# Values as the stationary operand in a branched attention, with the output scale brought in by two transfers

## The reference

```python
s = einsum('bqghd,bgqmd->bghqm', qb, k_sel) * scale
p = _masked_softmax(s - slopes * dist, dist >= 0)       # e / sum(e)
o_slc = einsum('bghqm,bgqmd->bqghd', p, v_sel)
...
o_win = einsum('bghqk,bkgd->bqghd', p_win, vw)
o = gb[..., 0:1] * o_cmp + gb[..., 1:2] * o_slc + gb[..., 2:3] * o_win
```

## Time and profile before

| | |
|---|---|
| median of 3 runs | 2609.11 us (2608.38 to 2610.36) |
| the profiled execution | 2607.89 us |
| its span | 2606.1 us |
| PE busy, 12947 products | 2545.3 us (98%) |
| DVE / ACT / POOL busy | 1198.0 / 833.9 / 1160.2 us |
| 16 DMA engines, mean | 86 GB/s |

### The profile page before, as it was taken

The page is one execution under the profiler, slowest core; times in us unless marked ns, Lnnn a source line. Parts: engine busy times, 40 slices in busy tenths (PEclk is TensorE's granted clock), DMA queues, the critical chain, the costliest instruction groups (busy, mean ns, idle before and its releaser), DMA issues.

```text
span 2606.1 us, 37755 instructions
## 1 busy us (share of the span) xinstructions
PE 2545.3 (98%) x12947; PEld 2158.3 (83%) x12947; DVE 1198.0 (46%) x2275; ACT 833.9 (32%) x1473; POOL 1160.2 (45%) x586
## 2 busy tenths in 40 slices
PE   7989999999999999999999999999999999999998
PEld 6788888887888888899888788888899888888887
DVE  6556666664432221177775422211477765322211
ACT  4456554664221110144444211100244443211101
POOL 4335430000277788700000777788300002877886
PEclk9989999999999999999999999999999999999999
DMA  7321113333233333322223233333222222333332
GB/s 161 107 41 34 33 42 81 89 89 89 87 97 97 97 95 98 102 66 77 70 83 92 81 97 97 97 97 97 90 78 73 65 87 81 95 96 96 98 95 76
DMA packets 422189, 222.88 MB, mean 86 GB/s; under 512 B 59504, under 2 KB 420268, under 8 KB 422060
## 3 DMA queue, kind: packets, MB, share of 16 engines
q1 hardware_dynamic: 419100, 218.03, 29.5%
q10 hardware_dynamic: 2960, 3.22, 0.4%
HBM read 212.86 MB, written 2.10 MB: 82 GB/s over the span
## 4 chain that ended last, share of the span: by engine, by line
PE 88%; DVE 7%; ACT 3%; issue 2%; DMA 0%; DVEq 0%; ACTq 0%; POOL 0%
PE psA L1063 48%; PE psB L1086 13%; PE psA L1086 10%; PE psA L1319 5%; PE psB L1319 4%; PE psO L967 3%; PE psB L948 2%; PE psB L924 1%; DVE b L2009 1%; DVE b L1669 1%; DVE b L2157 1%; ACT b L2460 1%; DVE b L2049 0%; PE psO L1359 0%; DVE b L2030 0%
## 5 line engine op out<-in xcount | busy, mean ns | idle before, releaser
L1063 PE MATMUL psA<-b,b 128*128 128x512 f32 x5616 | 1286.8, 391 | 3.8 <-DVE b L1458 1.8
L1063 PEld LDWEIGHTS psA<-b,b 128*128 128x128 f32 x5616 | 1054.1, 188 | 234.4 <-issue 8.9
L743 POOL TENSOR_TENSOR b<-b,b 128x1024 fp32r<-128x1024 f32 x239 | 453.5, 1897 | 1201.2 <-PE psA L1063 1041.1
L745 POOL TENSOR_TENSOR b<-b,b 128x1024 fp32r<-128x1024 f32 x239 | 594.1, 2486 | 18.7
L1086 PE MATMUL psB<-b,b 128*128 128x512 f32 (+4 forms) x1626 | 367.6, 384 | 7.7 <-DVE b L1893 4.5
L1086 PEld LDWEIGHTS psB<-b,b 128*128 128x128 f32 (+2 forms) x1626 | 299.6, 196 | 67.9 <-DVE b L1893 4.9
L1086 PE MATMUL psA<-b,b 128*128 128x512 f32 x1356 | 326.2, 396 | 0.0
L1458 DVE SCALAR_TENSOR_TENSOR b<-psA,b 128x512 f32<-128x512 f32 x152 | 104.7, 691 | 461.3 <-PE psA L1063 457.5
L1086 PEld LDWEIGHTS psA<-b,b 128*128 128x128 f32 x1356 | 253.3, 189 | 54.8 <-issue 1.0
L1469 DVE TENSOR_TENSOR b<-b,psA 128x512 f32 x48 | 33.0, 688 | 338.0 <-PE psA L1063 338.0
L2343 ACT ACTIVATE b<-b,b (+1 forms) x56 | 40.5, 724 | 441.1 <-DVE b L1469 434.6
(11 more groups left out here) (271 smaller groups left out, 2177.2 us busy)
## 6 DMA issues: line engine op xcount, KB each, us to landing
b<-in_w_in SPq DMA_DIRECT2D x296, 256.0 KB, 3.1
b<-in_w_ffn_in SPq DMA_DIRECT2D x176, 256.0 KB, 3.1
b<-in_w_ffn_out SPq DMA_DIRECT2D x64, 256.0 KB, 2.9
b<-in_w_out SPq DMA_DIRECT2D x48, 256.0 KB, 3.0
b<-in_w_gate SPq DMA_DIRECT2D x44, 256.0 KB, 3.1
b<-in_w_up SPq DMA_DIRECT2D x44, 256.0 KB, 3.2
b<-in_w_down SPq DMA_DIRECT2D x32, 256.0 KB, 3.0
b<-in_w_ffn_out SPq DMA_DIRECT2D x32, 192.0 KB, 2.5
```

Source lines behind the costliest of these rows:

```text
L743: nc.gpsimd.tensor_tensor(w[:, 0], wraw[:, s], ones[:, 0:1].broadcast_to([P, KT * P]), ALU.mult).then_inc(w_hi.sem, 1)
L745: nc.gpsimd.tensor_tensor(w[:, 1], wraw[:, s], hi_f(w[:, 0]), ALU.subtract).then_inc(w_lo.sem, 1)
L1063: i = mm(dst, w[:, wh, kt * P:(kt + 1) * P], rhs(xh, kt), start=first and kt == 0 and n == 0, stop=last and kt == kts - 1 and n == 2)
```

## The change

`values` keeps `vtok` (key tile by [high | low] columns) stationary and moves `PT`: for each key tile one product over all its queries, 512, 384, 256 and 128 columns, for both halves of `PT`. `psO` then has [high 64 | low 64] on the partitions and the 512 queries in the columns. The scale is therefore needed along the columns, equal on all partitions: `unit_scale` on SP waits for `gate`, writes the 128 x 4 numbers as a row of 512 into HBM, waits for that, and loads the row onto all 128 partitions (256 KB). `scaled` waits for that load. `gate(U + 1)` is placed where `gate(U)` was, `gate(0)` ahead of the loop. POOL adds only the two branches. `pair_output` adds high and low halves by two products with a constant "fold" matrix, whose moving operand is the added output, 512 columns in full precision. SP's order of query copies and weight loads is written anew around the `unit_scale` calls.

```diff
-                  ("slope", HEADS), ("edge", 32), ("lam", 4),
+                  ("slope", HEADS), ("edge", 32), ("lam", 4), ("fold", 3 * HD),
...
+    at = CONST["fold"].start
+    c[:, at + HD:at + 2 * HD] = (p % HD == np.arange(HD)[None])
...
-        om = pl(TT, 2, HD)
+        om = pl(T)
...
+        ow_row = [nc.dram_tensor(f"unit_scale{b}", (T,), F32).ap() for b in range(2)]
...
+        def scale_of(U):
+
+            if U >= 28:
+                return (n_r0, n_r2)[U % 2][:, :]
+            return hi_f(attnT[:, U % 2, 4 if U in (0, 2) else 6, :])
...
+            def unit_scale(U):
+
+                b, o = U % 2, 32 * (U % 2) + 16
+                sp.wait_ge(ug_dve.sem, ug_dve.at(U))
+                sp.dma_start(ow_row[b].rearrange("(q p) -> p q", p=P), st[:, o:o + TT], allow_slow_non_contiguous=True).then_inc(row_out[b], 16)
+                sp.wait_ge(row_out[b], 16 * (U // 2 + 1))
+                sp.dma_start(scale_of(U), ow_row[b].partition_broadcast(P)).then_inc(scale_in[b], 16)
...
-            for n in range(1, 4):
-                query_twice(n)
-                query_load(n + 4)
...
+            unit_scale(0)
+            for n in range(8):
+                unit_scale(4 * n + 1)
+                if n < 7:
+                    query_twice(n + 1, 0)
+                unit_scale(4 * n + 2)
+                if n < 7:
+                    query_twice(n + 1, 1)
+                if n < 3:
+                    query_load(n + 5)
+                else:
+                    lru_weights(n - 3)
+                unit_scale(4 * n + 3)
+                if n < 7:
+                    unit_scale(4 * n + 4)
+            for c in range(5, 4 * KT):
+                lru_weights(c)
...
-                nc.gpsimd.tensor_tensor(ow[0][:, :], ow[0][:, :], ow[1][:, :], ALU.add).then_inc(oa_pool.sem, 1)
-                pool.wait_ge(oa_pool.sem, oa_pool.at(j, "units"))
                 if hd == 0 and n:
                     pool.wait_ge(ot_pe.sem, ot_pe.at(n - 1))
-                parts = ow[0][:, :].rearrange("p (q h d) -> p q h d", h=2, d=HD)
-                nc.gpsimd.tensor_tensor(om[:, :, hd, :], parts[:, :, 0, :], parts[:, :, 1, :], ALU.add).then_inc(oa_pool.sem, 1)
+                nc.gpsimd.tensor_tensor((om, ow[1])[hd][:, :], ow[0][:, :], ow[1][:, :], ALU.add).then_inc(oa_pool.sem, 1)
...
-                    for qt in range(TT):
-                        for kt in range(qt + 1):
-                            at = PT_AT[kt] + (qt - kt) * P
-                            i = mm(psO[:, qt * P:(qt + 1) * P], PT[:, h, at:at + P],
-                                   vtok[:, br, kt, n // 4, hd, :, :].rearrange("p h d -> p (h d)"),
-                                   start=h == 0 and qt == 0, stop=h == 1 and kt == qt, skip_group_check=True)
+                    for kt in range(TT):
+                        at, w = PT_AT[kt], (TT - kt) * P
+                        i = mm(psO[:, T - w:T], vtok[:, br, kt, n // 4, hd, :, :].rearrange("p h d -> p (h d)"),
+                               PT[:, h, at:at + w], start=h == 0 and kt == 0, stop=h == 1 and kt == TT - 1, skip_group_check=True)
...
-                for qt in range(TT):
-                    i = mm(psO[:, qt * P:(qt + 1) * P], om[:, qt, :, :].rearrange("p h d -> p (h d)"), ident,
-                           start=False, stop=qt == TT - 1, skip_group_check=True)
+                for hd in range(2):
+                    at = CONST["fold"].start + (1 - hd) * HD
+                    i = mm(psO[:, :], con[:, at:at + P], (om, ow[1])[hd][:, :], start=False, stop=hd == 1, skip_group_check=True)
...
-                o = 32 * (U % 2)
                 dve.wait_ge(uv_pe.sem, uv_pe.at(U))
-                dve.wait_ge(ug_dve.sem, ug_dve.at(U))
-                if U >= 2:
-                    dve.wait_ge(oa_pool.sem, oa_pool.at(U // 2 - 1, "units" if U % 2 else "parts"))
-                v.tensor_tensor(ow[U % 2][:, :].rearrange("p (q c) -> p q c", c=P), psO[:, :].rearrange("p (q c) -> p q c", c=P),
-                                st[:, o + 16:o + 20].unsqueeze(2).broadcast_to([P, TT, P]), ALU.mult).then_inc(uo_dve.sem, 1)
+                dve.wait_ge(scale_in[U % 2], 16 * (U // 2 + 1))
+                if U % 4 == 1 and U > 4:
+                    dve.wait_ge(ot_pe.sem, ot_pe.at(U // 4 - 1))
+                elif U >= 2:
+                    dve.wait_ge(oa_pool.sem, oa_pool.at(U // 2 - 1))
+                v.tensor_tensor(ow[U % 2][:, :], psO[:, :], scale_of(U), ALU.mult).then_inc(uo_dve.sem, 1)
...
-                gate(U)
+                if U + 1 < 32:
+                    gate(U + 1)
...
+            gate(0)
             for n in range(8):
```

More of the change, by code:

```diff
@@ L447, in build @@
         uo_dve = steps("unit_scaled", ["all"])
-        oa_pool = steps("head_added", ["units", "parts"])
+        oa_pool = steps("head_added", ["units"])
+        row_out = [sem(f"unit_scale_row_stored{b}") for b in range(2)]
+        scale_in = [sem(f"unit_scale_loaded{b}") for b in range(2)]
         cs_pe = steps("compressed_scores", ["all"])
@@ L629, in _, with query_twice @@
                     load(c, c % RAW, [(b, b + 2, w1[:, 4 * s + b:4 * s + b + 2, :]) for b in (0, 2)], wide_rows)
-            def query_twice(n):
-                for hd in range(2):
-                    here, there = (slice(b * HD, (b + 1) * HD) for b in (hd, 1 - hd))
-                    sp.wait_ge(ql_pool.sem, ql_pool.at(n, f"lo{hd}"))
-                    q = query_pair(n, hd)
-                    sp.dma_start(hi_f(q[there, :, :]), hi_f(q[here, :, :])).then_inc(q_twice[hd], 16)
-            query_twice(0)
+            def query_twice(n, hd):
+                here, there = (slice(b * HD, (b + 1) * HD) for b in (hd, 1 - hd))
+                sp.wait_ge(ql_pool.sem, ql_pool.at(n, f"lo{hd}"))
+                q = query_pair(n, hd)
+                sp.dma_start(hi_f(q[there, :, :]), hi_f(q[here, :, :])).then_inc(q_twice[hd], 16)
+            def unit_scale(U):
[4 more added lines that the diff above has]
+                sp.dma_start(scale_of(U), ow_row[b].partition_broadcast(P)).then_inc(scale_in[b], 16)
+            query_twice(0, 0)
+            query_twice(0, 1)
             for n in range(2, 5):
                 query_load(n)
-            for n in range(1, 4):
-                query_twice(n)
-                query_load(n + 4)
             o3 = 2608
@@ L650, in lru_load, with lru_weights @@
                 load(C_LRU + c, c % RAW, parts, dst)
-            for m in range(KT):
-                for x in range(3):
-                    if m == 0:
-                        query_twice(x + 4)
-                    lru_load(4 * m + x, col_tile(w_in, KT, m * P + o3 + x * D))
-                if m == 0:
-                    query_twice(7)
-                lru_load(4 * m + 3, [(b, 0, woa[b, :, :, m * P:(m + 1) * P]) for b in range(2)],
-                         lambda slot, b: slot[b * HD:(b + 1) * HD, :, :])
+            def lru_weights(c):
+                m, x = divmod(c, 4)
+                if x < 3:
+                    lru_load(c, col_tile(w_in, KT, m * P + o3 + x * D))
+                else:
+                    lru_load(c, [(b, 0, woa[b, :, :, m * P:(m + 1) * P]) for b in range(2)],
+                             lambda slot, b: slot[b * HD:(b + 1) * HD, :, :])
+            unit_scale(0)
[8 more added lines that the diff above has]
+                    query_load(n + 5)
+                else:
+                    lru_weights(n - 3)
[4 more added lines that the diff above has]
+                lru_weights(c)
             def gate_load(m):
```

## The result

The changed kernel takes **2783.4 us** (median of 4 runs, 2780.3 to 2787.1) against 2609.1: ratio 1.067, with a 95% interval of [1.065, 1.068], 174 us slower.

The account below looks back on a forecast made before the run. TensorE was taken to set the attention's pace, busy 29.7 of a group's 30.1 us. Shorter work -26, clock -6 and transfers +2 gave -30 us from 2609.1: 2579 us, forecast 2570 to 2588, range 2563 to 2600.

Parts of the forecast that it names:

- The two transfers: Each unit's gate to HBM and back over all partitions: 4.2 to 9.2 us, taken as 6; 2 us charged in all.
- Rival 4: Transfers set the attention's pace, two units taking the chain plus 6.0 us; at 11 us chain 22 us slower, 2631; chance 0.08.
- The cover: Time from the gate's place to the scaling that needs it: 9.8 and 8.6 us, about 7 left to hide the transfers.
- over 7 us together: Stated failure condition: the forecast falls if a unit's two transfers together take more than 7 us.
- Values: A unit's twenty value products become eight: block 1.25 us, 0.94 less; second and third units get all of it.
- Fold: Per group, four passes of 512 columns replace eight of 128: 0.43 us each, 0.83 us more in the second unit.
- Gate: Reciprocal and gate a unit earlier: ScalarE's copy less late, at most 1.3 us in first units, about 0.4 in fourth.
- VectorE's share: VectorE's busy part of an attention group was to rise from 71% to 79% and meet some of the gain.
- rival 1: The chain stays: copy and subtraction end no earlier because VectorE becomes the bound; gain 17, 2592 us; chance 0.22.
- Clock: Of 17.7 us lost to TensorE's reduced clock in the attention, 6 us come back; ends 0 and 12.
- rival 3: TensorE's clock gets worse, half-clock time doubling from 40 us and costing 20: 2605 us, no change; chance 0.10.
- Moves at no cost: Fewer GpSimd additions, reordered SP query copies and weight loads, a row-reading scaling: free; larger constants 0 to 0.5 us.

Follow-up runs that it names:

- run 6: Changed kernel with its 512 four-byte pieces written at a pitch of 8 bytes, eight per 64 bytes instead of sixteen: 2595.8 us, one run.
- experiment 1: Changed kernel without its two transfers, the scaling multiplying by a constant row instead: 2572.4 us, ratio 0.985 to the kernel before.
- experiment 12: Changed kernel with 16-byte pieces and partition-major order kept to the pair's end, undone by strided PSUM reads: 2574.1 us, ratio 0.9855 to the kernel before.

## Why the prediction was wrong

**The step that failed is "The two transfers".** It bounded the pair of transfers by 4.2 to 9.2 us and took 6, with the reason "the second being like the 3.0 row and the first no larger in packets". The rows that it used (2.1, 3.0 and 4.6 us) are transfers into SBUF, none of them writes to HBM, and none has pieces of four bytes. The upper end was thus no bound at all. Measured: 11.9 + 5.4 = 17.3 us against a cover of about 7, and a loss of 211 us where 2, at most 8, were charged. What the runs showed in its place: 512 four-byte pieces dense in HBM land 7.2 us after their last packet, and SP, which waits in order, passes each landing on to the next unit.

**Rival 4 named the mechanism and the sign; its chance of 0.08 and its price were too low.** Its argument against itself, "4.6 us is the slowest row of comparable size", compared sizes where the density of the pieces decides. Its formula, two units in the chain plus 6.0 us, would give (17.3 + 6.0) / 2 = 11.7 us per unit for the measured chain; 13.0 were measured. It let the two parities overlap. They can't, since SP waits for the first transfer of one unit before it issues that of the next, which the SP rows show. The text spoke of SP's wait between the two transfers, but did not count whom it keeps waiting on that queue. At 32 units, 5.26 us over the old 7.78 make the 168. No run issued the transfers of the two parities from two queues, so how much of the loss is the slow landing and how much the order on SP is not separated.

The rival's thresholds are also off by its own rows. With a forecast of 26.9 us for a clean group, two units take 13.45, so the chain decides above about 7.4 us, not 6; and against the clean 15.1 us that it compares with, a chain of 11 us costs 30 us, not the 22 that come from mixing it with the average of 7.8. Neither would have brought the measured time near.

**The cover was there, for a transfer of normal length.** With pieces of 16 bytes the pair takes 2.3 + 3.6 = 5.9 us, as forecast, and the best version loses 1.7 us to the one without transfers, which fits the 2 charged and can't be told from nothing. At 8.0 us together (run 6) 20 us are lost, so "over 7 us together" was a fair limit.

**Values: the block right, its worth not.** A block takes 1.22 us start to start, 1.25 forecast. But the lower end of 2.1 us per clean group, shorter blocks and the fold with the copies as late as before, was 0.45 when run alone (30.1 to 29.65): the prediction let the second and third units get all of it, and together they took 16.6 us as before, behind the wait for the reciprocal.

**Fold: right.** 0.43 us from one pass to the next.

**Gate: right in kind, and its part grew.** The wait for the reciprocal goes. Alone it gains 0.94 per clean group; beside the shorter products it is worth 2.9 (29.65 to 26.74). The sum added parts that in fact need each other. The total came out right (8 x 3.36 = 27 us, 26 forecast), but with the products priced too high alone and the gate too low beside them; that the two errors cancel is partly luck.

**VectorE's share:** 21.0 of 26.74 us, 79% as forecast, and the chain did not stay: rival 1 falls.

**Clock: more came back than forecast.** By the prediction's own measure the half-clock time falls from 40 us to 15 (28.89 x 0.12 + 28.26 x 0.06 + 26.03 x 0.07 + 22.87 x 0.02, twice). Beyond those 27 us the attention of experiment 1 shortens by 9 more (249.0 to 213.0), against 6, within the 0 to 12. So 38 us came where 32 (26 and 6) were summed. In the changed kernel it is the other way: clocks of 0.73 to 0.80 in all eight groups, which is rival 3's sign, "group clocks below those of the earlier trace rows". There it follows from the waits: without the transfers the same program reads 1.00 in four groups.

**Moves at no cost: right in themselves.** In experiment 12 the clean groups are as in experiment 1, and the query copies take 2.9 us as before. In the changed kernel the query copies stand behind slow transfers on the same queue (6.9 us instead of 2.9), and TensorE waits 40 us for them.

**The signs it gave were the right ones.** It named waits of the scaling for L656 as rival 4's sign and "over 7 us together" as what would make it fall, and the profile after shows both.

## What to carry to other kernels

Here a transfer of 2 KB was priced by how densely its four-byte pieces land in HBM, not by its bytes: write each partition's results as 16 bytes in one piece (2.3 us instead of 11.9), or leave space between the pieces (2.4), and undo the order where it was free, when VectorE or ScalarE reads PSUM. A duration from a transfer into SBUF did not bound this write to HBM; without a row of the same kind and direction, the upper end is open and the rival that hangs on it deserves more than a tail. And where a queue waits in its own order for each transfer, the landing sets the period of the loop once it is the longest step, although there are two buffers here (13.0, 11.8 and 11.3 us per unit at landings of 11.9, 10.0 and 9.5). Two parts of one change may also need each other: test each alone before giving each a price.

## What was not expected of the hardware

- 512 writes of four bytes, dense in 2 KB of HBM: 11.9 us to land; 64 bytes apart 2.4, as 128 pieces of 16 bytes 2.3. The packets' own records end 7.2 us (median) before the landing, so the records alone don't show the cost; the time from issue to landing does.
- VectorE over 512 columns: SBUF operand read at a stride of 16 bytes 1079 ns, SBUF output written in steps of 512 bytes 1074, against 686 to 692 when only the PSUM operand is strided (in steps of 512 bytes). ScalarE's copy from PSUM at a stride of 16 bytes: 598 ns, as contiguous.
- TensorE, full precision over 512 columns: 1078 ns with a moving operand strided by 16 bytes, 592 contiguous.
